# Strassen's seven block products for three of four gate-pair blocks, and eight token sums moved between the gate halves

## What is computed

```python
def trunk_layer(x, past, ...):
    proj = x @ w_in + b_in
    (q_a, k_a, v_a, g_a, q_b, k_b, v_b, g_b, q_i, k_i, w_i, r_a, r_b) = jnp.split(proj, _split_points(), axis=-1)
    ...
    y_a = stick_breaking(q_a, k_a, v_a, q_pos, k_pos)        # 8 heads, strictly causal
    y_b = sparse_attention(q_b, k_b, v_b, q_i, w_i, k_i, ...)  # indexer top-k, then softmax
    y_a = y_a.reshape(b, t, W_A) * jax.nn.silu(g_a)
    y_b = y_b.reshape(b, t, W_B) * jax.nn.silu(g_b)
    merged = jax.nn.sigmoid(r_a) * (y_a @ w_pa) + jax.nn.sigmoid(r_b) * (y_b @ w_pb)
    x = layer_norm(ALPHA * x + merged @ w_out, ln_g, ln_b)
    return x, new_rows
```

## Time and profile before

| | |
|---|---|
| Median of 3 runs | 1025.94 us (1025.83 to 1026.34) |
| The profiled execution, its own time | 1025.23 us |
| Its span, first to last instruction | 1023.4 us |
| Mean granted TensorE clock | 0.994 |
| Busy share of PE, PEld, DVE, ACT, POOL | 96%, 88%, 72%, 50%, 58% |
| Merge stage, layer 0 | 310.93 to 464.65 us |
| Merge stage, layer 1 | 811.04 to 964.07 us |

### The profile page before, as it was taken

How to read it: one execution, slowest core, us unless ns; L and a number is a source line. 1 busy time by engine, 2 the same in 40 slices (tenths; PEclk the granted TensorE clock), 3 DMA queues, 4 the chain that set the end, 5 groups by cost and what they waited for, 6 DMA issues and landing times.

```text
span 1023.4 us, 18526 instructions
## 1 busy us (share of the span) xinstructions
PE 982.2 (96%) x7240; PEld 898.4 (88%) x7240; DVE 740.9 (72%) x1333; ACT 515.0 (50%) x908; POOL 590.0 (58%) x494
## 2 busy tenths in 40 slices
PE   6999999999999999999999999999999999989997
PEld 5889997778899999998788999777888999989985
DVE  7479998879953767438965899978898338745347
ACT  6564326668957333343235633466788543444320
POOL 2436556536556768688524365555465469587650
PEclk9999999999999999999999999999999999999998
DMA  7512542111112222255243125301111221231622
GB/s 239 187 56 80 168 148 88 43 36 44 47 42 71 78 65 78 83 192 198 88 164 110 43 95 170 129 2 43 42 43 42 83 63 64 81 116 50 233 77 93
DMA packets 71163, 96.51 MB, mean 94 GB/s; under 512 B 4498, under 2 KB 62340, under 8 KB 70436
## 3 DMA queue, kind: packets, MB, share of 16 engines
q1 hardware_dynamic: 67124, 83.74, 25.3%
q0 software_dynamic: 3776, 11.50, 3.3%
q10 hardware_dynamic: 176, 0.07, 0.0%
HBM read 82.09 MB, written 14.79 MB: 95 GB/s over the span
## 4 chain that ended last, share of the span: by engine, by line
PE 71%; DVE 15%; POOL 9%; ACT 3%; issue 2%; DMA 0%; DVEq 0%; ACTq 0%; POOLq 0%
PE ps L673 18%; PE ps L1054 12%; PE ps L987 10%; PE ps L1106 7%; PE ps L902 4%; DVE attn L1776 4%; DVE attn L1749 3%; DVE top L1773 3%; PE ps L704 3%; POOL w_lo L2280 2%; PE ps L923 2%; PE ps L881 2%; PE ps L962 2%; PE ps L941 2%; PE ps L863 2%
## 5 line engine op out<-in xcount | busy, mean ns | idle before, releaser
L2161 POOL TENSOR_TENSOR w_lo<-raw,w_hi 128x512 fp32r<-128x512 f32 x83 | 115.2, 1388 | 250.1 <-ACT w_hi L1153 249.9
L673 PE MATMUL ps<-xT_hi,w_hi 128*128 128x288 f32 x608 | 180.9, 298 | 2.7 <-POOL w_lo L2162 2.7
L673 PE MATMUL ps<-xT_hi,w_lo 128*128 128x288 f32 x608 | 179.1, 295 | 0.0
L673 PE MATMUL ps<-xT_lo,w_hi 128*128 128x288 f32 x608 | 179.0, 294 | 0.0
L2162 POOL TENSOR_TENSOR w_lo<-raw,w_hi 128x512 fp32r<-128x512 f32 x83 | 124.9, 1505 | 0.0
L673 PEld LDWEIGHTS ps<-xT_hi,w_hi 128*128 128x128 f32 x608 | 114.1, 188 | 4.3 <-POOL w_lo L2162 3.6
L673 PEld LDWEIGHTS ps<-xT_lo,w_hi 128*128 128x128 f32 x608 | 114.1, 188 | 0.0
L673 PEld LDWEIGHTS ps<-xT_hi,w_lo 128*128 128x128 f32 x608 | 114.0, 188 | 0.0
L1153 ACT ACTIVATE w_hi<-raw 128x1024 fp32r<-128x1024 f32 (+1 forms) x84 | 87.6, 1044 | 38.2 <-PE ps L673 17.8
L2280 POOL TENSOR_TENSOR w_lo<-raw,w_hi 128x512 fp32r<-128x512 f32 x56 | 75.8, 1364 | 35.8 <-ACT w_hi L1509 35.6
L2255 POOL TENSOR_TENSOR attn<-attn 128x1024 f32<-128x1024 f32 (+1 forms) x24 | 54.3, 2261 | 54.8 <-DVE attn L1884 54.8
(11 more groups left out here) (286 smaller groups left out, 3029.0 us busy)
## 6 DMA issues: line engine op xcount, KB each, us to landing
raw<-in_w_in SPq DMA_DIRECT2D x44, 1024.0 KB, 5.2
raw<-in_w_out SPq DMA_DIRECT2D x8, 1024.0 KB, 5.1
x_kept<-x_nat SPq DMA_DIRECT2D x2, 2560.0 KB, 10.5
x_nat<-x_kept SPq DMA_DIRECT2D x2, 2560.0 KB, 10.2
raw<-in_w_proj_a SPq DMA_DIRECT2D x8, 512.0 KB, 3.5
raw<-in_w_proj_b SPq DMA_DIRECT2D x8, 512.0 KB, 4.6
x_nat<-in_x_prompt SPq DMA_DIRECT2D x4, 512.0 KB, 5.3
out<-stage POOLq DMA_DIRECT2D x8, 256.0 KB, 4.8
```

Of the source, the lines that this page charges most:

```text
L673: last = mm(out, a, b[:, HALF * half:HALF * (half + 1)], start=(k == 0 and i == 0), stop=(k == n - 1 and i == 2))
L2161: g.tensor_tensor(lo[:, 0:half, :], src[:, 0:half, :], hi[:, 0:half, :].bitcast(f32), ALU.subtract)
```

## The change

J0 becomes 1. So groups J = 1, 2, 3 go by seven products instead of J = 2, 3, and only group 0 is plain. As t1 to t4 are now wanted earlier, token-sum steps 0 to 7 move into the stick-breaking stage, between the gate halves 11 to 15 (`SUMS_AT`). t24, which holds t2 and then t4, gets a place of its own in place of one in x_nat; it lies over the second half of w_sums and the start of bias_near. Low parts move from POOL to DVE: of y six are now DVE's and two POOL's, and all low parts of merged are DVE's. DVE waits for `s_lo` ahead of the y parts (`low_parts_of`) until POOL has made the low parts of RB 0 and RB 1. The PR products of m = 2, 3 come in quarters, as those of m = 4 to 7 did.

```diff
-J0 = 2
+J0 = 1
...
+SUMS_AT = {11: (0,), 12: (1, 2, 3), 13: (4,), 14: (5, 6, 7)}
...
+        with nc.sbuf_tensor("first_sums", [128, 2, 4, 128], f32), nc.sbuf_tensor("t24", [128, 4, HALF], f32) as t24:
             pass
...
                         if J == J0 and kind == "RA" and i == 1:
-                            pe.wait_ge(s_tf, L * 14 + 11)
+                            pe.wait_ge(s_tf, L * 14 + 10)
+                        if J == J0 and kind == "RA" and i == 5:
+                            pe.wait_ge(s_tf, L * 14 + 13)
...
                     y_head(act, L, Y_ORDER[2 * n + 3])
+                    if n == 0:
+                        act.wait_ge(s_gate, L * 8 + 8)
+                        token_sum_hi(t1_hi[:, :, :], t1[:, :, :], 3)
+                    elif n == 1:
+                        token_sum_hi(t2_hi[:, :, :], t24[:, :, :], 8)
+                        token_sum_hi(t3_hi[:, :, :], t3, 6)
...
                     if 1 in steps:
                         if P:
                             dve.wait_ge(s_qlo_w, L * NQ + quarter_of_pair(P - 1) + 6)
+                        else:
+                            dve.wait_ge(s_tf, L * 14 + 14)
...
                     for n in HALVES_AT[p - 1]:
                         gate_half(n)
+                        for i in SUMS_AT.get(n, ()):
+                            token_sum(i)
...
+                def merged_lo(m):
+
+                    dve.wait_ge(s_mhi, L * 8 + m + 1)
+                    merged = qy[:, sig_slot("RA", m), :]
+                    v.tensor_tensor(late_m_lo[:, m, :], merged[:, 0:SEQ],
+                                    late_m_hi[:, m, 0:SEQ].bitcast(f32), ALU.subtract)
+                    v.tensor_tensor(late_m_both[:, m, DEC:2 * DEC], merged[:, SEQ:TOK],
+                                    late_m_hi[:, m, SEQ:TOK].bitcast(f32), ALU.subtract).then_inc(s_mlo, 1)
+
+                def low_parts_of(u):
+                    dve.wait_ge(s_lo, L * T0 + u + 2)
+
+                low_parts_of(U[("RB", 0)])
+                y_rest(2)
+                y_rest(3)
+                low_parts_of(U[("RB", 1)])
+                y_rest(4)
+                y_rest(5)
+                token_sum(8)
+                token_sum(9)
+                y_rest(6)
+                y_rest(7)
+                token_sum(10)
+                token_sum(11)
+                token_sum(12)
+                merge(0, (0,))
                 weight_sums("RA", J0, (0,))
-                merge(2)
+                merge(0, (1, 2))
+                token_sum(13)
+                merge(1, (0,))
                 weight_sums("RA", J0, (1,))
-                merge(3, (0,))
+                merge(1, (1,))
                 for J in range(J0, 4):
                     combine("RA", J, (0,))
-                    if J == J0:
-                        last_token_sum_lo()
                     weight_sums("RB", J, (0,))
                     combine("RA", J, (1,))
                     weight_sums("RB", J, (1,))
                     combine("RA", J, (2,))
-                    combine("RB", J, (0, 1, 2))
+                    merged_lo(2 * J - 2)
+                    combine("RB", J, (0,))
+                    merged_lo(2 * J - 1)
+                    combine("RB", J, (1, 2))
                     merge(2 * J)
...
-                def merged_rest(m):
-
-                    pool.wait_ge(s_mhi, L * 8 + m + 1)
...
                     for Q in range(q + 4, q + 18):
                         quarter_rest(Q)
-                        if Q in (q + 6, q + 8):
-                            merged_rest(2 * J - 2 + (Q - q - 6) // 2)
```

More of the change, by code:

```diff
@@ L694, in dense @@
                         return
[L695 to L698, removed]
+                    wait_evacuated(GROUP[u])
                     if kind == "QI":
@@ L1947, in last_token_sum_lo @@
[L1947 to L1950 removed]
+                        token_sum_step(n, t3, t3, b12[1], ALU.subtract)
+                    elif n == 6:
+                        token_sum_step(n, t24[:, :, :], b22[0], t1[:, :, :], ALU.subtract)
+                    elif n == 7:
+                        token_sum_step(n, t24[:, :, :], t24[:, :, :], b22[1], ALU.add)
+                    elif n == 8:
+                        dve.wait_ge(s_th, L * 4 + 1)
+                        token_sum_step(n, t1_lo[:, :, :], t1[:, :, :], t1_hi[:, :, :].bitcast(f32), ALU.subtract)
+                    elif n == 9:
+                        dve.wait_ge(s_th, L * 4 + 2)
+                        token_sum_step(n, t2_lo[:, :, :], t24[:, :, :], t2_hi[:, :, :].bitcast(f32), ALU.subtract)
+                    elif n == 10:
+                        token_sum_step(n, t24[:, :, :], b21[0], t24[:, :, :], ALU.subtract)
+                    elif n == 11:
+                        token_sum_step(n, t24[:, :, :], t24[:, :, :], b21[1], ALU.add)
+                    elif n == 12:
+                        dve.wait_ge(s_th, L * 4 + 3)
+                        token_sum_step(n, t3_lo[:, :, :], t3, t3_hi[:, :, :].bitcast(f32), ALU.subtract)
+                    else:
+                        dve.wait_ge(s_th, L * 4 + 4)
+                        token_sum_step(n, t4_lo[:, :, :], t24[:, :, :], b12[0], ALU.subtract)
@@ L1984, in combine @@
                     if 0 in steps:
-                        dve.wait_ge(s_mlo, L * 8 + 2 * J - 2)
+                        if J == 1:
+                            dve.wait_ge(s_ylo_v, L * 6 + 6)
+                        else:
+                            dve.wait_ge(s_mlo, L * 8 + 2 * J - 2)
                         dve.wait_ge(s_qdone, q0 + 1)
@@ L2114, in _ @@
                         weight_sums("RA", J + 1, (0, 1))
-                    merge(2 * J + 1, (0,) if J < 3 else (0, 1))
+                        merge(2 * J + 1, (0, 1))
+                merge(7, (0,))
+                merged_lo(6)
+                merge(7, (1, 2))
+                merged_lo(7)
                 if L == 0:
@@ L2264, in _ @@
                     rest(N_G + 2 + n)
-                def y_rest(i):
-                    pool.wait_ge(s_yhi, L * 8 + Y_ORDER.index(i) + 1)
+                for n in range(2):
+                    i = Y_ORDER[n]
+                    pool.wait_ge(s_yhi, L * 8 + n + 1)
                     g.tensor_tensor(late_y_lo[:, i, :], qy[:, y_row(i), :], late_y_hi[:, i, :].bitcast(f32),
```

114 lines of the change are left out of this document (36 added, 78 removed).

## The result

The changed kernel takes **1015.06 us** (median of 4 runs, 1014.38 to 1015.65), the kernel before 1025.95 in its 4 runs beside them. The ratio is **0.9893, 95% interval 0.9876 to 0.991**. The forecast was 1010, its range 1005 to 1018, the forecast's own range 1007 to 1013. So the kernel got faster by 11 us where 16 were forecast, and the question is where the other 5 are.

The account below looks back on a forecast made before the run. PE, 96% busy, was taken to bound the kernel, its late-layer waits set by POOL sharing SBUF with DVE. 1025.2 - 6.4 - 12.5 (steps 2, 4, 5) + 3.2 = 1009.5, median 0.7 higher: 1010 us; own range 1007 to 1013, with rivals 1005 to 1018.

Parts of the forecast that it names:

- step 6: Third product of pair RB: new PE wait for DVE's copy, behind the merged low part; +3.2 us in all (0 to 7.4).
- Step 1: Two more Strassen pairs per layer remove 48 matmuls of 288 columns in all: -6.4 us, called certain.
- Step 2: Eight token sums moved into gate halves: the 1.4 us wait before PR2 per layer goes; new cost taken as 0.
- Step 3: Four low parts of y moved to DVE's idle 11.4 us between the gating and its last y parts: cost 0.
- Step 4: Strassen pairs: PE's waits of 2.4 and 0.8 us on POOL's low parts go, and the slow clock with them.
- Step 5: Output projection, layer 0: the 0.9 us wait goes, since POOL has 3 us less to do ahead of wo_lo.
- Step 7: Further PSUM combinations, weight sums and POOL low parts, with ACT and DMA having room: no cost.
- the shared resource still sets the pace: Rival: SBUF work shared by DVE and POOL keeps waits at J = 1 and PR1; 1016.5 us, chance 0.23.

Follow-up runs that it names:

- number 9: Kernel before plus six token sums in the gate halves and low parts of merged tiles 2 to 7 on DVE behind the copy, no further products: 1013.85 us.
- number 1: Changed kernel with the copy of bank 0 in pair RB ahead of the low part of merged tile 2J-2: 1008.1 us, repeated at 1006.8 us.
- number 7: Kernel before with only token sums 0 to 5 moved between the gate halves: 1023.7 us, ratio 0.9978.
- number 8: Changed kernel with all eight token sums taken out of the gate halves and put behind the gating: 1040.1 us, ratio 1.0136.
- number 6: Changed kernel with the four moved low parts of y back on POOL: 1016.8 us, ratio 0.9914.
- number 5: Changed kernel with the low parts of merged tiles 0 to 5 back on POOL at their old places: 1013.9 us, ratio 0.9886.
- number 2: Changed kernel with only the 128x64 instruction of tile 2J-2's low part moved behind the copy: 1008.0 us, ratio 0.9824.
- number 3: Changed kernel with one more 128x64 subtraction, its output unread, ahead of the copy: 1020.6 us, ratio 0.9947.
- number 4: Changed kernel with one input of the 128x64 instruction ahead of the copy read from PSUM instead of SBUF: 1008.4 us, ratio 0.9833.

## Why the prediction was right or wrong

Of the seven steps one was badly mis-sized, step 6. The measured 1015.06 us lies outside the forecast's own range of 1007 to 1013, and above the 1014.4 that the upper bound of step 6 gives; it lies in the stated range of 1005 to 1018 because that was drawn to take in a rival whose mechanism did not come. That much is luck.

- **Step 1, products, -6.4: right.** 48 matmuls fewer (7240 to 7192), and 7.0 us between numbers 9 and 1 on one chip.
- **Step 2, sums in the gate halves: right.** The waits before PR2 went, no wait came at the gate halves, and the lateness was taken up. Alone it brought 1.9 us (number 7), and its cover is real (number 8).
- **Step 3, y parts at no cost: right**, and a little better than claimed: left on POOL, they would have cost 1.75 us (number 6), because then they meet DVE's token sums.
- **Step 4, waits in the pairs and the slow clock: right.** No w_lo wait in the merge stage, and no window there with a clock of 0.50. Number 5 brings POOL's waits back (8.3 us in its six groups).
- **Step 5, output projection: half right.** The 0.9 us in layer 0 went. In layer 1 a wait of 0.45 shown came, which the prediction didn't have; start to start it is 981.99 to 982.83 where a step takes 0.23, so 0.6 us. Its cause is open: the profiled executions of numbers 1 to 5 and 8 don't have it, in number 6 it is 0.2, so it may belong to this one execution.
- **Step 6 is the one that failed, in size.** The wait was named with its place (third product of pair RB, copy behind merged_lo, 14.3 us after the pair's start) but priced 3.2 us; it measures **7.7**, a little above its upper bound of 7.4. Nor is it longest at J = 1, as forecast: 1.19 us there, 1.32 at J = 2 and 3. Two sentences of it were wrong. "The worst order is not the rule: 0.3" took POOL being busy four fifths of the time as a chance that the order is kind. The order is not drawn by lot: at this place POOL has an instruction running each time, so each DVE instruction with two SBUF inputs waits for the one that runs, and the low part is two instructions. 2.96 us came every time, at J = 2 and 3 as at J = 1. And the last combination comes later than the J = 3 of the earlier trace rows: the weight sum ahead of it took 1.78 us for the same reason, so the combination waits no longer for PE. That left about 1.6 us of the 2.2 us that were to hide the low part. 2.96 - 1.6 = 1.4 a pair is what the rows show (1.2 to 1.3). I had counted the shared path in busy time per pair, which says whether POOL keeps up, and had not asked how long one DVE instruction takes to get through.
- **Step 7, the rest at no cost: not contradicted**; pair RA of J = 1 runs without a gap in PE, with DVE at 10.33 of 11.13 us. POOL's 128x512 instructions in the groups take 1.4 to 1.5 us on the mean, under the 1.6 that would have spoken against it.

Worked through again with the measured terms, span against span: -6.4 - 11.0 - 1.5 + 7.7 + 0.6 = -10.6 us; the spans differ by -10.0. The 0.6 left over is of the size of the 0.56 us by which the changed kernel is late already at 286 us, ahead of everything that the edit touches.

Of the rivals, "the shared resource still sets the pace" gave 1016.5, near the time, but by POOL waits of 2.4 at J = 1 and 1.4 at PR1 that did not come; numbers 1 and 2 decide against it. It cited the Trainium skill, "Perfetto Trace Analysis", section "Optimizing Scalar/DVE Operations": moving work between VectorE and GpSimd might not help. In this case that depended on the place: the low parts moved to DVE and placed behind the copy brought 5.8 us (number 1 against 5), moved and placed ahead of it nothing (1015.1 against 1013.9).

**The better version** is number 1: the same instructions with one low part three lines further down, 1008.1 and 1006.8 us, 0.981 of the kernel before. All six copy waits go, and what is left of PE's waits lies outside the merge stage and the output projection.

## What to carry to other kernels

Where DVE and POOL share SBUF work, count DVE's instructions with two SBUF inputs that stand ahead of something PE waits for, and charge each a whole POOL instruction, however short it is, unless POOL has a gap there; then put them behind it, or let one input come from PSUM. A busy-time sum tells whether the two keep up, not when one instruction gets through. And when an edit takes a wait away, follow what now stands first in its queue: here the order of two lines was worth as much as the 48 products.

## What the runs showed of the hardware

- A DVE subtraction of 128x64 with both inputs in SBUF takes 0.21 us in a gap of POOL (number 3, 402.55) and 1.29 beside POOL; with one input in PSUM it takes 0.21 beside POOL too (number 4).
- The clock does not always fall after the same wait. Behind 2.24 us of idle PE in number 3 it fell in layer 1 and stayed in layer 0, as behind 2.26 in the kernel before it fell in layer 0. The stretches behind the two waits where it fell cost about 1.5 us each.
- Much of the spread between runs of one kernel seems to be such stretches at other places. The five runs of number 1 go from 1004.9 us (mean clock 0.998) to 1009.1 (0.993), and the slowest, which is the profiled one, has two of them in stages that the edit doesn't touch, the first behind 0.73 us of idle time and the second behind waits of 1.06 and 0.20 (windows of PE):

```profile
212.00:214.00 2.00, 2.00 (x12) 0.50 0.03 8
...
519.00:522.00 3.00, 3.00 (x14) 0.50 1.01 431
```

So single runs of this kernel tell apart nothing under some 4 us, and the comparisons above rest on medians and intervals.
